# Latent attention laid out anew: memory queries from x before the norm, memory heads between the projections, group data in three buffers, the query's norm factor in the exponential

## The reference

```python
for i in range(DEPTH_2):
    h = rmsnorm_2(x, norm_mix[i])
    ...                                   # i == 0: fox, i == 1: mla
    o_mem = memory_cross(p[..., -MEM_WIDTH:], k_mem, v_mem, mem_q_gain[i], mem_k_gain[i])
    x = x + jnp.concatenate([o_mix, o_mem], axis=-1) @ w_out[i]
    x = x + conv_ffn(rmsnorm_2(x, norm_ffn[i]), ffn_w_up[i], ...)

def mla_mixer(p, cos, sin, qa_norm, kva_norm, w_q_up, w_kv_up, q_gain, k_gain):
    q_lat, kv_lat, k_r = jnp.split(p, [MLA_Q_RANK, MLA_Q_RANK + MLA_KV_RANK], axis=-1)   # 256, 128, 32
    q = (rmsnorm_2(q_lat, qa_norm) @ w_q_up).reshape(b, s, 12, 96)
    kv = (rmsnorm_2(kv_lat, kva_norm) @ w_kv_up).reshape(b, s, 12, 64 + 64)
    q = jnp.concatenate([q[..., :64], rope(q[..., 64:], cos, sin)], axis=-1)
    k_rope = jnp.broadcast_to(rope(k_r[:, :, None, :], cos, sin), (b, s, 12, 32))
    k = jnp.concatenate([kv[..., :64], k_rope], axis=-1)
    v = kv[..., 64:]
    q = rmsnorm_2(q, q_gain).transpose(0, 2, 1, 3) * 96 ** -0.5
    k = rmsnorm_2(k, k_gain).transpose(0, 2, 1, 3)
    return from_heads(causal_block_attention(q, k, v.transpose(0, 2, 1, 3)))
```

## The time and the profile before

| what | value |
|---|---|
| median of 3 runs | 1645.74 us (1643.57 to 1646.56) |
| the profiled execution | 1643.91 us |
| its span, first to last instruction | 1642.2 us |
| PE busy | 1565.1 us, 95% of the span |
| DVE, ACT, POOL busy | 825.2, 713.0, 334.9 us |
| mean granted clock of PE | 0.984 of full speed |

### The profile page before, as it was taken

One profiled execution on the slowest core, in us unless ns is written; L12 is line 12 of the kernel. 1 busy time (PEld: TensorE's weight loads), 2 busy tenths in 40 slices (PEclk: granted clock), 3 DMA queues, 4 the chain that ended last, 5 costly groups with the idle time before them and its releaser, 6 DMA issues. The chain is left out here.

```text
span 1642.2 us, 21202 instructions
## 1 busy us (share of the span) xinstructions
PE 1565.1 (95%) x8594; PEld 1312.0 (80%) x8594; DVE 825.2 (50%) x1341; ACT 713.0 (43%) x1309; POOL 334.9 (20%) x271
## 2 busy tenths in 40 slices
PE   7988998899999999999999999888899999999999
PEld 6777787799889788788888887666788788888887
DVE  5345444656444664755334442557764745334442
ACT  4435535356663544544224343455545534123431
POOL 0000133100340002244013431032102243014320
PEclk9999989899999999999999999989999999999999
DMA  6212112133231002233223331110002333223331
GB/s 223 78 33 83 52 52 65 40 141 114 79 104 38 27 1 77 90 103 109 96 78 102 99 119 56 45 55 16 24 1 88 92 91 125 85 84 93 110 106 52
DMA packets 37314, 128.49 MB, mean 78 GB/s; under 512 B 4176, under 2 KB 8928, under 8 KB 37216
## 3 DMA queue, kind: packets, MB, share of 16 engines
q1 hardware_dynamic: 37216, 127.13, 23.9%
HBM read 125.01 MB, written 2.10 MB: 77 GB/s over the span
## 5 line engine op out<-in xcount | busy, mean ns | idle before, releaser
L309 PE MATMUL bank<-hhi,whi 128*128 128x512 f32 (+1 forms) x1072 | 422.5, 394 | 4.3 <-DVE wlo L301 3.3
L311 PE MATMUL bank<-hhi,wlo 128*128 128x512 f32 (+1 forms) x1072 | 418.5, 390 | 0.0
L310 PE MATMUL bank<-hlo,whi 128*128 128x512 f32 (+1 forms) x1072 | 418.2, 390 | 0.0
L301 DVE TENSOR_TENSOR wlo<-wstage,whi 128x1024 fp32r<-128x1024 f32 (+3 forms) x206 | 273.7, 1332 | 145.5 <-ACT whi L290 145.1
L290 ACT CAST whi<-wstage 128x1024 fp32r<-128x1024 f32 (+3 forms) x206 | 228.8, 1116 | 136.7 <-PE bank L311 128.5
L309 PEld LDWEIGHTS bank<-hhi,whi 128*128 128x128 f32 (+1 forms) x1072 | 200.9, 187 | 50.1 <-DVE wlo L301 5.4
L2283 DVE SCALAR_TENSOR_TENSOR cr<-bank,vc,cr 128x511 f32<-128x511 f32 (+1 forms) x168 | 125.8, 749 | 218.4 <-ACT cr L2223 215.4
L311 PEld LDWEIGHTS bank<-hhi,wlo 128*128 128x128 f32 (+1 forms) x1072 | 200.6, 187 | 43.8
L310 PEld LDWEIGHTS bank<-hlo,whi 128*128 128x128 f32 (+1 forms) x1072 | 200.8, 187 | 42.6 <-issue 0.6
L2223 ACT ACTIVATE cr<-bank,vc 128x512 f32<-128x512 f32 x84 | 65.5, 780 | 249.8 <-PE bank L311 249.8
L2325 POOL TENSOR_TENSOR cr<-cr,cr 128x512 f32<-128x512 f32 x44 | 94.2, 2140 | 312.1 <-DVE cr L2283 277.4
(11 more groups left out here) (416 smaller groups left out, 2337.8 us busy)
## 6 DMA issues: line engine op xcount, KB each, us to landing
wstage<-in_wts SPq DMA_DIRECT2D x148, 512.0 KB, 3.5
wstage<-in_wts SPq DMA_DIRECT2D x32, 704.0 KB, 4.1
wstage<-in_wts SPq DMA_DIRECT2D x18, 768.0 KB, 4.3
xT<-in_x SPq DMA_DIRECT2D x4, 512.0 KB, 5.0
xt<-in_x SPq DMA_DIRECT2D x4, 512.0 KB, 5.6
out<-ob SPq DMA_DIRECT2D x8, 256.0 KB, 2.3
U<-in_rel_ext SPq DMA_DIRECT2D x6, 256.0 KB, 9.3
wstage<-in_wts SPq DMA_DIRECT2D x3, 384.0 KB, 3.0
```

The lines of the kernel that those rows point to most:

```text
L301: e.tensor_tensor(K.wlo[i % 3][:, 0:w], K.stage[i % 3][:, 0:w], K.whi[i % 3][:, 0:w].bitcast(F32), SUB).then_inc(*K.dve.up(("wlo", i)))
L309: e.matmul(o, lh, rh, start=start, stop=False)
L310: e.matmul(o, lh, rl, start=False, stop=False)
L311: return e.matmul(o, ll, rh, start=False, stop=stop)
```

## The change

- **norm2.** ffn0's last 8 steps also form x times gain with high and low part (`act_scaled`, `dve_scaled`, 8 instructions each on ACT and DVE). `norm2` now works as the other two: PE makes the two memory-query tiles from these (`pe_norm`), DVE divides them after (`divided`, into `mqT1`). The barrier `bar6` stands ahead of `norm2`.
- **All three norms** take two steps: the two products come one after the other instead of side by side, and a weight chunk may be split between k-tile 3 and 4 of the norm's elementwise work.
- **lat** makes its chunks one by one; the sums of squares stand within the following product. The squares have a ring of two buffers of their own, `tmpl`.
- **Schedule.** The items of the memory heads stand among `lat`, `group0` and `group1`, where they stood behind `lat` and `group0`; group 2 begins two items ahead of the first latent head. Groups 0 and 1 use PSUM banks 7 and 3, scores of this layer 3 banks (0 to 2), and bank 3 alone serves group 2 and the turned q and k of every head.
- **Preparation of a head**: q at step t0-4 and k at t0-3, each behind that step's maximum, exponential and copy, where both were at t0-2 ahead of them.
- **Factor of the queries.** POOL no longer multiplies the queries; the factor is the `scale` of the exponential on ACT, and DVE multiplies the maximum by it (new `TENSOR_TENSOR` of 128x1 behind each of the 48 maxima of latent items). The keys are multiplied by POOL in four instructions, one per head.
- **Group buffers**: three pairs of `qt`, `kt`. The gains are loaded in ffn0.
- **Layer 0's attention**: at most one split between two of its steps, at 7 places (after 0, 20, 26, 32, 38, 44 and 50 steps) instead of 5 (0, 20, 28, 36, 44).

```diff
@@ due
-    if not SPLITS[g]:
+    if not SPLITS[g] or (made and SCHEDULE[g] in ("foxatt", "mlaatt")):
         return False
@@ Attention.prep
         for h, t0 in self.first.items():
-            if t + 2 == t0:
-                return self.heads[h].prep
+            if self.heads[h].prep is not None and t - t0 in (-4, -3):
+                return self.heads[h].prep, "qk"[t - t0 + 4]
@@ pe_att
-            for which in ("q", "k"):
-                name, src, nz = A.prep(t)(which)
-                b = A.T.take(q, (name, "T"))
+            prep, which = A.prep(t)
+            name, src, nz = prep(which)
+            b = A.R.take(q, (name, "T"))
@@ act_att, soft
-        e.activation(p[:, 0:n], src[:, 0:n], ACT.Exp, bias=A.mx[:, h, i:i + 1], accum_out=A.rs[:, h, i:i + 1]).then_inc(
+        factor = 1.0
+        if A.heads[h].factor:
+            factor, made = A.heads[h].factor(i)
+            q.wait_ge(*K.at(made))
+        e.activation(p[:, 0:n], src[:, 0:n], ACT.Exp, bias=A.mx[:, h, i:i + 1], scale=factor,
+                     accum_out=A.rs[:, h, i:i + 1]).then_inc(
@@ dve_att, soft
+            if factor:
+                f, made = factor(i)
+                q.wait_ge(*K.at(made))
+                q.wait_ge(*K.at((A.name, "mx0", t)))
+                e.tensor_tensor(m, m, f, MUL).then_inc(*K.dve.up((A.name, "mx", t)))
@@ pe_norm, new for all three
+    x = Parts(("u", s), *K.xu)
+    K.RA.go_on_at(0)
+    for n, key in enumerate(PAIRS[s]):
+        i, hi, lo = K.chunk(q, *key)
+        o = K.RA.take(q, key)
+        for k in range(8):
+            q.wait_ge(*K.at((x.gen, "hi", k)))
+            q.wait_ge(*K.at((x.gen, "lo", k)))
             z = mm3(e, o[:], hi[:, k, :], lo[:, k, :], x.hi[:, k, :], x.lo[:, k, :], k == 0, k == 7)
+            if n == 0 and k == 1:
+                pe_sum_whole(e, q, K, s, 7)
+        z.then_inc(*K.pe.up(key, K.used(i)))
+        yield
@@ pool_group
-    scale("k", kt, rk)
...
-    scale("q", qt, rq)
+    for h in range(4):
+        x = kt[:, :, h, :]
+        q.wait_ge(*K.at(("k", j, "r")))
+        q.wait_ge(*K.pool.last())
+        e.tensor_tensor(x, x, rk[:, h:16:4].unsqueeze(2).to_broadcast([P, 4, 96]), MUL).then_inc(
+            *K.pool.up(("k", j, "normed", h)))
@@ schedule
-    out += ["out0"] + ["foxatt"] * 3 + ["out0"] * 7 + ["bar5", "norm1"] + ["ffn0"] * 63 + ["norm2", "bar6"]
-    out += ["lat"] * 5 + ["group0"] * 8
-    side = {}
-    for t0, n, name in ((-1, 9, "group0"), (7, 17, "group1")):
-        for s in range(n):
-            side.setdefault(t0 + s, []).append(name)
-    for s in range(17):
-        side.setdefault(27 + (s // 2 if s < 8 else s - 4), []).append("group2")
-    for t in range(-2, 69):
-        out += ["mlaatt"] + side.get(t, [])
-    out += ["out1"] + ["mlaatt"] * 3 + ["out1"] * 7 + ["bar7", "norm3"] + ["ffn1"] * 64
+    out += ["out0"] + ["foxatt"] * 3 + ["out0"] * 7 + ["bar5"] + ["norm1"] * 2 + ["ffn0"] * 63 + ["bar6"] + ["norm2"] * 2
+    out += ["lat"] * 3 + ["mlaatt"] * 2 + ["lat"] + ["mlaatt"] * 2 + ["lat"]
+    out += ["group0", "group0", "mlaatt"] * 4
+    for n in range(8):
+        out += ["group0"] * (n < 6) + ["group1", "mlaatt"]
+    for t in range(14, 69):
+        out += ["group1"] * (t < 20) + ["group2"] * (t in (14, 15, 18, 19, 22, 23, 26, 27) or 28 <= t < 34) + ["mlaatt"]
+    out += ["out1"] + ["mlaatt"] * 3 + ["out1"] * 7 + ["bar7"] + ["norm3"] * 2 + ["ffn1"] * 64
@@ memory of the rings
+    K.RQ, K.RH, K.RS3 = (Ring(K, b, K.in_bank) for b in (banks[3:4], [banks[7], banks[3]], banks[0:3]))
```

More of the change, by code:

```diff
@@ L1136, in act_att @@
             act_evac(e, q, K, (A.name, "pt", t - 3), (A.name, "T", t - 3), o[:, 0:n], K.bank((A.name, "T", t - 3))[:, 0:n])
+        if A.prep(t):
+            prep, which = A.prep(t)
+            name, scale, r = prep(which + "h")
+            hi = K.mring[which].take(q, name)
+            for x in r:
+                q.wait_ge(*K.at(x))
+            q.wait_ge(*K.at((name, "T")))
+            e.activation(hi[0][:], K.bank((name, "T"))[0:96, :], ACT.Identity, scale=scale).then_inc(*K.act.up((name, "hi")))
         p = A.post(t)
@@ L1848, in dve_norm @@
     low(7)
-    if pair is not None:
-        for key in first_pair(pair):
-            q.wait_ge(*K.at(first_pair(pair)[1]))
-            e.tensor_tensor(divided(K, pair, key), K.bank(key)[:], K.hold["rb", s][:], MUL).then_inc(
-                *K.dve.up((key, "made"), frees=[key, ("rb", s)]))
+    for key in PAIRS[s]:
+        q.wait_ge(*K.at(PAIRS[s][1]))
+        e.tensor_tensor(divided(K, s, key), K.bank(key)[:], K.hold["rb", s][:], MUL).then_inc(
+            *K.dve.up((key, "made"), frees=[key, ("rb", s)]))
     yield
@@ L2438, in pe_lat, with sums @@
     x = Parts("h3", K.hhi, K.hlo)
-    def sums(name, j, start, stop, take):
-        if take:
-            K.RO.take(q, name)
-        q.wait_ge(*K.at(("lsq", j)))
-        z = e.matmul(K.bank(name)[:], K.ones[:], K.tmp["lsq", j][:], start=start, stop=stop)
-        z.then_inc(*K.pe.up(name if stop else (name, j), frees=[("lsq", j)]))
-    pe_pair(e, q, K, LAT[0:2], x, 8, T, K.RS)
-    sums(("lsum", 0), 0, True, False, True)
-    sums(("lsum", 0), 1, False, True, False)
-    yield
-    pe_fm(e, q, K, LAT[2], x, 8, T, K.RS)
-    sums(("lsum", 1), 2, True, True, True)
-    yield
-    pe_fm(e, q, K, ("kr", 0), x, 8, T, rows=32)
+    def sums(name, js, ring):
+        b = ring.take(q, name)
+        for j in js:
+            q.wait_ge(*K.at(("lsq", j)))
+            z = e.matmul(b[:], K.ones[:], K.tmp["lsq", j][:], start=j == js[0], stop=j == js[-1])
+            z.then_inc(*K.pe.up(*[name] * (j == js[-1]), frees=[("lsq", j)]))
+    pe_fm(e, q, K, LAT[0], x, 8, T)
+    yield
+    pe_fm(e, q, K, LAT[1], x, 8, T)
+    for m in range(2):
+        o = K.RA.take(q, ("mms", m))
+        q.wait_ge(*K.at(("mmsq", m)))
+        e.matmul(o[:], K.blk[:], K.tmp["mmsq", m][:], start=True, stop=True).then_inc(
+            *K.pe.up(("mms", m), frees=[("mmsq", m)]))
+    yield
+    pe_fm(e, q, K, LAT[2], x, 8, T, mid=lambda: sums(("lsum", 0), (0, 1), K.STAT))
+    yield
+    K.RA.go_on_at(4)
+    pe_fm(e, q, K, ("kr", 0), x, 8, T, rows=32, mid=lambda: sums(("lsum", 1), (2,), K.RA))
+    yield
+    K.RA.go_on_at(3)
     b = K.RA.take(q, "krT")
@@ L2485, in norm @@
             q.wait_ge(*K.at(("ln", j)))
-            e.copy(K.lhi[:, j, :], K.tmpd["ln", j][:]).then_inc(*K.act.up(("lhi", j)))
+            e.copy(K.lhi[:, j, :], K.tmpl["ln", j][:]).then_inc(*K.act.up(("lhi", j)))
+    for m in range(2):
+        t = K.tmp.take(q, ("mmsq", m))
+        q.wait_ge(*K.at((("mm", m), "made")))
+        e.activation(t[:], K.mqT1[:, m, :], ACT.Square).then_inc(*K.act.up(("mmsq", m)))
+    yield
     square(0)
+    yield
     square(1)
+    for m in range(2):
+        t = K.tmp.take(q, ("mmr", m))
+        q.wait_ge(*K.at(("mms", m)))
+        act_rstd(e, q, K, ("mmrs", m), t[:], K.bank(("mms", m))[:], 64, frees=[("mms", m)])
     norm(0, (0, 1))
@@ L2540, in dve_lat @@
     yield
-    t = K.tmpd.take(q, "kr")
+    t = K.tmpl.take(q, "kr")
     q.wait_ge(*K.at(("kr", 0)))
```

319 lines of the change are left out of this document (133 added, 186 removed).

## The result

The changed kernel takes 1681.93 us (median of 4 runs, 1681.58 to 1682.85) against 1644.95 (4 runs beside it, 1643.57 to 1646.56): 1.0225 times as long, interval 1.0208 to 1.0243. I had forecast +6.6 us, and it is +37. The direction was right, the size was not: the time lies far above the range of 1635 to 1662.

The account below looks back on a forecast made before the run. PE, busy 95% of the span, was taken as the bound, time changing only by its waits or lower clock; -2.4 + 1.1 + 1.5 + 6.1 + 0.3 - 1 + 1 = +6.6 us, 1652.3 on the median, range 1635 to 1662.

Parts of the forecast that it names:

- Part A: Norm2 and lat: waits and lower clock worth 6.85 us go, new waits and moved work come; -2.4 us in sum.
- D: Steady latent heads, six in the window: `mql` on bank 3 and VectorE's queue make a pair 17.2 us; +6.1 us.
- C: First five latent heads: less query-tile work, but PE's idle time grows from 9.6 to some 13.2; +1.5 us.
- B: Memory heads between projections: 11.9 us of waits and lower clock go, 11.4 of new waits and 1.6 come; +1.1 us.
- R1: The forecast itself: VectorE's queue paces the latent heads at about 8.6 us; 1648 to 1658 us, chance 0.44.
- The clock: Lower-clock stretches at norm2 and the memory heads go, worth 1.65 and 4.5 us; products between new waits keep full clock.
- the rule: Clock-gate page: short matmul bursts with waits between hold the array at its lower level; 4.5 us more at the memory heads.
- R4: Rival: the clock stays at the lower level between memory-head steps, 4.5 to 6 us more; 1657 to 1660 us, chance 0.10.
- The rest: Last head's exponentials +0.3 us, layer 0's attention -1, norm1 and norm3 +0.5 each.
- My signs: Expected profile marks, such as 17.2 us a pair; wrong if a pair takes 15 or less or first latent score precedes 1108.

Follow-up runs that it names:

- e1_prep_first: Changed kernel with high and low parts of the turned q and k put ahead of the step's exponential, maximum and copy; 1660.07 us.
- e2_no_factor: Changed kernel without the factor: POOL multiplies the queries again, the 48 multiplications on VectorE and the exponentials' column scale are gone; 1669.0 us.
- e7_k_later: Changed kernel with the turned k of a head at step t0-2 instead of t0-3; 1659.5 us.
- e3_filled: Changed kernel with 190 extra score matmuls filling PE's waits ahead of the turned k of each latent head but the first; 1667.8 us.
- e4_before_factor: Kernel before with the factor alone: column scale in the latent exponentials, VectorE multiplies the maximum, POOL no longer the queries; 1655.89 us.

## Why the prediction was wrong

**Part A** held: -2.6 for -2.4. The wait inside the first latent product came as several of 0.4 to 0.5 for `hhi`, 1.3 together for 1.9, the one at the rotary keys as 2.3 for 2.8.

**The waits** were sized right in D, not in C. PE's idle time, window less busy, changed as follows (forecast, measured): A -1.3, -2.5; B +4.0, +2.3; C +3.6, +9.7; D +6.1, +6.2; in all +12.7, +16.1. That the whole comes this near is in part luck, since A and B fell short where C ran over, and since the lower clock hides some of the waiting. In D the first pair, almost all at full clock, took 16.7 us (7.84 and 8.89) and a pair of the filled kernel 17.6, for 17.2; the other pairs of the changed kernel, with the lower clock in them, took 19.9 and 20.7. The mechanism of R1, `mql` behind a maximum, a multiplication and an exponential on the one bank, is what e1_prep_first, e2_no_factor and e7_k_later show: each widens that distance or shortens that chain, and 13 to 22 us come back. The term of C was mis-sized: my walk had 13.2 us of idle time in the five heads, and 19.3 were measured. At the turned k of heads 2 and 4 alone the waits were 4.5 and 5.4 us; ahead of them VectorE had the split of a weight chunk (1.47 us from 1133.54, 1.23 from 1162.25) and, in the second, group 2's sums (three of 0.54 to 0.55) in front of the maximum on which `mql` hangs.

**The clock** is the step that failed. The sum had it as a gain, 1.65 at norm2 and 4.5 at the memory heads, together -6.1. Measured, PE's busy time rose by 22.8 us: 28.9 us between the two, against 3.4 between the forecast waits and the measured ones. The failing sentence is in part B: "I take the latter, since the products between these waits are longer than the steps in the row's stretch". I weighed the rule only there and priced it in R4 at 4.5 to 6 us for one stretch. It had to stand beside every wait that I found: in D I had worked out 1 us or more per head and left the clock at 1.00. The trace of before agreed with the rule already, at 0.50 behind the 4.1-us wait. e3_filled shows that the low clock has a price of its own, since added matmuls made the kernel 14 us faster; that is the part of the 22.8 that came back, and with it 23 of the 37 us stayed. The Trainium skill's page "TensorE: Matmul & The Clock Gate", section "HAM oscillation — how this bites in real kernels", tells of an array that falls back to the lower level at every wait between bursts of matmuls. This case agrees in part: its clock fell again and again (0.76 and 0.86 in the two stretches), at waits of 2.3 us on the mean, but not behind every wait.

**The rest**: layer 0's attention was forecast at -1 and came at +1.4. Its wait did shrink from 3.54 to 2.4 us as said, but the array was at 0.50 from 545 to 549 us behind it, and its stretch before had been at 0.64 for 4 us. Norm1 came at +0.5, as forecast. 2.5 us of the +4.4 stand ahead of any edit, in code that is the same in both; the profile of e4_before_factor, which is the kernel before up to the latent part, is 2.5 us behind that of the kernel before at the start of norm2 too. Head 11 and what follows cost 4.5 for 0.8: the 20 us from head 11's first score on ran at 0.81, where they had been at 1.00.

**My signs** were of use for the mechanism only. The waits at L1080 for `mql`, 0.16 and 0.78 for the two operations, and a pair near 17 us at full clock were found. But none of the signs of being wrong came up (a pair of 15 or less, other times for the two operations, a first score before 1108), and the forecast was 30 us off: they all looked to the faster side, and none named the clock. VectorE was busy for 66% of the steady stretch (37.76 of 57.38 us), where I had said some 85%; so "VectorE's queue paces the heads" holds only for where the queue stands, in front of the 512-wide maximum, and not as an engine that is full. And the first latent score, forecast at about 1113, stood at 1120.3: 4.4 of it came from ahead of norm2, the rest from part B, whose clock was 0.82 where I had put 1.00.

**Two slips** in the working change nothing above: R4's 4.5 to 6 us on top of 1652.3 give 1657 to 1658, not 1657 to 1660; and POOL loses six long multiplications, three of queries and three of keys, for the twelve short ones.

## What to carry to other kernels

A wait on the matrix engine had two prices here: its own length, and slower products behind some of the waits. Whoever adds waits that come back with every head must price both. Here PE's busy time rose by 22.8 us and its idle time by 16.1, and 14 of the 37 us came back when the waits were filled. When a step is moved ahead so that its result is early, look at the order within the step too: what matters is how far the last reader of a shared bank stands from the next writer, and one exchange of order on ScalarE and VectorE was worth 22 us.
